# Head pairs of a fused three-layer kernel: later source tiles added on VectorE before the products with a constant -1 matrix

## What is computed

```python
z = jnp.einsum('bhqd,bhkd->bhqk', qb, kb).astype(jnp.float32) * SB_SCALE
mask = k_pos < q_pos
log_1m_beta = jnp.where(mask, -jax.nn.softplus(z), 0.0)
suffix = lax.cumsum(log_1m_beta, axis=3, reverse=True) - log_1m_beta
w = jnp.where(mask, jnp.exp(jax.nn.log_sigmoid(z) + suffix), 0.0)
outs.append(jnp.einsum('bhqk,bhkd->bhqd', w.astype(vb.dtype), vb))
```

## Time and profile before

| | before |
|---|---|
| median of 3 runs (lowest to highest) | 1312.52 us (1311.21 to 1314.37) |
| the profiled execution: its time, and its span | 1313.82 us, 1312.1 us |
| PE busy | 1266.3 us, 97% of the span |
| DVE, ACT, POOL busy | 645.4, 572.5, 398.7 us |
| granted clock of PE, mean | 0.986 of full speed |
| head stage: from its first DVE instruction to its end | 763.4 to 1029 us, eight steps of 33.0 or 33.7 us |

### The profile page before, as it was taken

The page is one execution under the profiler, slowest core; times in us unless marked ns, Lnnn a source line. Parts: engine busy times, 40 slices in busy tenths (PEclk is TensorE's granted clock), DMA queues, the critical chain, the costliest instruction groups (busy, mean ns, idle before and its releaser), DMA issues.

```text
span 1312.1 us, 19522 instructions
## 1 busy us (share of the span) xinstructions
PE 1266.3 (97%) x7802; PEld 1049.3 (80%) x7802; DVE 645.4 (49%) x1208; ACT 572.5 (44%) x1086; POOL 398.7 (30%) x194
## 2 busy tenths in 40 slices
PE   6999998999989999999999999999999999999998
PEld 5799876998968766656699988887877888888898
DVE  6373054485884646789847133333333391102534
ACT  4435313443331227688856343545354311434333
POOL 1454301224544211110020432222222354444441
PEclk9999998999989999999999999999999999999999
DMA  5322200733584331110012331212122223233221
GB/s 174 125 70 91 96 1 32 257 111 119 174 225 83 66 79 33 33 33 1 2 33 69 93 95 60 61 56 64 57 65 63 90 98 94 90 98 111 82 91 65
DMA packets 130209, 109.68 MB, mean 84 GB/s; under 512 B 36162, under 2 KB 127424, under 8 KB 130128
## 3 DMA queue, kind: packets, MB, share of 16 engines
q1 hardware_dynamic: 130128, 108.54, 27.9%
HBM read 106.43 MB, written 2.10 MB: 83 GB/s over the span
## 4 chain that ended last, share of the span: by engine, by line
PE 68%; issue 18%; POOL 7%; DVE 4%; ACT 2%; DMA 0%; POOLq 0%; DVEq 0%; ACTq 0%
PE banks L1135 33%; POOL w_lo L565 6%; PE banks L1126 6%; PE banks L1158 5%; PE banks L1683 3%; PE banks L1535 3%; PE banks L1552 3%; PE banks L1567 3%; PE banks L1223 2%; PE banks L1590 2%; PE banks L1646 2%; PE banks L1697 1%; PE banks L1727 1%; PE banks L1102 1%; DVE w_lo L1793 1%
## 5 line engine op out<-in xcount | busy, mean ns | idle before, releaser
L565 POOL TENSOR_TENSOR w_lo<-raw,w_hi 128x1024 fp32r<-128x1024 f32 x158 | 388.1, 2478 | 821.7 <-ACT w_hi L638 821.6
L1135 PE MATMUL banks<-act_hi,w_hi 128*128 128x512 f32 x704 | 280.8, 399 | 5.8 <-POOL w_lo L565 5.8
L1135 PE MATMUL banks<-act_hi,w_lo 128*128 128x512 f32 x704 | 276.1, 392 | 0.0
L1135 PE MATMUL banks<-act_lo,w_hi 128*128 128x512 f32 x704 | 276.0, 392 | 0.0
L638 ACT ACTIVATE w_hi<-raw 128x1024 fp32r<-128x1024 f32 x168 | 168.1, 1050 | 145.0 <-PE banks L1135 98.7
L1135 PEld LDWEIGHTS banks<-act_hi,w_hi 128*128 128x128 f32 x704 | 133.4, 189 | 36.0 <-issue 8.7
L1135 PEld LDWEIGHTS banks<-act_hi,w_lo 128*128 128x128 f32 x704 | 133.4, 190 | 28.4 <-issue 1.4
L1135 PEld LDWEIGHTS banks<-act_lo,w_hi 128*128 128x128 f32 x704 | 133.3, 189 | 28.3
L1126 PE MATMUL banks<-w_hi,act_hi 128*128 128x256 f32 x384 | 109.1, 284 | 0.0
L1126 PE MATMUL banks<-w_hi,act_lo 128*128 128x256 f32 x384 | 108.7, 283 | 0.0
L1126 PE MATMUL banks<-w_lo,act_hi 128*128 128x256 f32 x384 | 108.7, 283 | 0.0
(11 more groups left out here) (362 smaller groups left out, 2441.0 us busy)
## 6 DMA issues: line engine op xcount, KB each, us to landing
raw<-w_in SPq DMA_DIRECT2D x32, 1024.0 KB, 5.7
raw<-gla_w_in SPq DMA_DIRECT2D x13, 1024.0 KB, 5.3
ada_raw<-w_ada SPq DMA_DIRECT2D x8, 1024.0 KB, 5.7
raw<-nsa_w_in SPq DMA_DIRECT2D x32, 256.0 KB, 4.6
raw<-nsa_w_in SPq DMA_DIRECT2D x7, 1024.0 KB, 5.1
raw<-gla_w_out SPq DMA_DIRECT2D x4, 1024.0 KB, 8.1
ada_first<-w_ada SPq DMA_DIRECT2D x4, 1024.0 KB, 7.3
raw<-nsa_w_out SPq DMA_DIRECT2D x16, 256.0 KB, 4.6
```

Of the source, the lines that this page charges most:

```text
L565: pool.tensor_tensor(w_lo[:, u, k], raw[:, u, k], w_hi[:, u, k].bitcast(F32), ALU.subtract).then_inc(lo_done, 1)
L1135: mm = pe.matmul(b[:], w[:, u, k, m * P:(m + 1) * P], x[:, k, :], start=(k == 0 and n == 0), stop=(k == KT - 1 and n == 2))
```

## The change

On DVE, the sums over later source tiles are made in float32 as soon as groups 1 and 2 are ready: `last_two` is tile 2 plus tile 3 for query tile 3; `later` has two query tiles for source tile 0: for query tile 2 it is tile 1 + tile 2, for query tile 3 tile 1 + `last_two`. They are split into parts, and only then group 0 gets its softplus. On PE every earlier zone takes one product with `minus_r` for each query tile and part instead of one for each later tile: 16 products of 128 columns and 4 of 256 instead of the 24. The products with `tri_r` are the same 16. The new tiles lie in memory that is free in this stage (the last tile of `br_lo` and `br_hi`, and `rstd`).

```diff
+        later = over("later", [P, 2, 2, P], br_lo, at=br_lo.manual_sbuf_range[1] - 4 * S)
+        later_lo = over("later_lo", [P, 2, 2, P], br_lo, F32R, at=br_lo.manual_sbuf_range[1] - 4 * S)
+        later_hi = over("later_hi", [P, 2, 2, P], br_hi, F32R, at=br_hi.manual_sbuf_range[1] - 4 * S)
+        last_two = over("last_two", [P, 2, P], rstd)
...
                 pe.wait_ge(sp_ready, 3 * (p + 1))
-                for jt in range(TT - 1, -1, -1):
-                    for a in range(2):
-                        for st in range(jt, -1, -1):
-                            for n, part in enumerate((sp_hi, sp_lo)):
-                                mm = pe.matmul(blocks(z_banks, a, st, skip=jt - st), (tri_r if jt == st else minus_r)[:],
-                                               blocks(part, a, jt), start=False, stop=(jt == st and n == 1), skip_group_check=True)
-                    if jt < TT - 1:
-                        mm.then_inc(tri_full, 1)
...
+                own(3)
+                sums(lambda a: column(a, 2, 3), minus_r, piece(3, 3))
+                own(2)
+                sums(lambda a: column(a, 1, 2), minus_r, piece(2, 2)).then_inc(tri_full, 1)
+                sums(lambda a: column(a, 1, 3), minus_r, [lambda a, x=x: x[:, a] for x in (last_two_hi, last_two_lo)])
+                own(1)
+                sums(lambda a: column(a, 0, 1), minus_r, piece(1, 1)).then_inc(tri_full, 1)
+                sums(lambda a: column(a, 0, 2, 2), minus_r,
+                     [lambda a, x=x: x[:, a].rearrange("p t n -> p (t n)") for x in (later_hi, later_lo)])
+                own(0).then_inc(tri_full, 1)
...
-                    dve.tensor_tensor(group(sp_lo, g), group(ln_z, g), group(sp_hi, g).bitcast(F32),
-                                      ALU.subtract).then_inc(sp_ready, 1)
...
+                softplus(0, 1)
+                softplus(1, 2)
+                if p:
+                    dve.wait_ge(tri_full, 3 * p)
+                tile2 = ln_z[:, 4].rearrange("p (a t n) -> p a t n", a=2, t=2)
+                link(dve.tensor_tensor(last_two[:], tile2[:, :, 1], ln_z[:, 2:4, 3 * P:], ALU.add))
+                dve.tensor_tensor(later[:, :, 0], tile2[:, :, 0], ln_z[:, 2:4, P:2 * P], ALU.add)
+                link(dve.tensor_tensor(later[:, :, 1], last_two[:], ln_z[:, 2:4, 2 * P:3 * P], ALU.add))
+                softplus_low(1).then_inc(sp_ready, 1)
+                softplus_low(2).then_inc(sp_ready, 1)
+                dve.tensor_copy(last_two_hi[:], last_two[:])
+                link(dve.tensor_copy(later_hi[:], later[:]))
+                dve.tensor_tensor(last_two_lo[:], last_two[:], last_two_hi[:].bitcast(F32), ALU.subtract)
+                link(dve.tensor_tensor(later_lo[:], later[:], later_hi[:].bitcast(F32), ALU.subtract))
+                softplus(2, 0)
+                softplus_low(0).then_inc(sp_ready, 1)
```

More of the change, by code:

```diff
@@ L238, in build_program @@
         w_z = over("w_z", [P, 5, S], sp_hi)
+        later = over("later", [P, 2, 2, P], br_lo, at=br_lo.manual_sbuf_range[1] - 4 * S)
+        later_lo = over("later_lo", [P, 2, 2, P], br_lo, F32R, at=br_lo.manual_sbuf_range[1] - 4 * S)
+        later_hi = over("later_hi", [P, 2, 2, P], br_hi, F32R, at=br_hi.manual_sbuf_range[1] - 4 * S)
+        last_two = over("last_two", [P, 2, P], rstd)
+        last_two_lo = over("last_two_lo", [P, 2, P], rstd, F32R)
+        last_two_hi = over("last_two_hi", [P, 2, P], rstd, F32R, at=last_two.manual_sbuf_range[1])
         pool_u = over("pool_u", [P, KT, S], qh)
@@ L1678, in head_sums, with sums, own, column @@
                 pe.wait_ge(sp_ready, 3 * (p + 1))
-                for jt in range(TT - 1, -1, -1):
-                    for a in range(2):
-                        for st in range(jt, -1, -1):
-                            for n, part in enumerate((sp_hi, sp_lo)):
-                                mm = pe.matmul(blocks(z_banks, a, st, skip=jt - st), (tri_r if jt == st else minus_r)[:],
-                                               blocks(part, a, jt), start=False, stop=(jt == st and n == 1), skip_group_check=True)
-                    if jt < TT - 1:
-                        mm.then_inc(tri_full, 1)
+                def sums(zones, weights, hi_lo, last=False):
+                    for n, part in enumerate(hi_lo):
+                        for a in range(2):
+                            mm = pe.matmul(zones(a), weights[:], part(a), start=False, stop=(last and n == 1),
+                                           skip_group_check=True)
+                    return mm
+                def own(st):
+                    return sums(lambda a: blocks(z_banks, a, st), tri_r,
+                                [lambda a, x=x: blocks(x, a, st) for x in (sp_hi, sp_lo)], last=True)
+                def column(a, st, first, n=1):
+                    at, c0 = zone(a, st)
+                    return z_banks[:, at, c0 + (first - st) * P:c0 + (first - st + n) * P]
+                def piece(st, first):
+                    def of(x, a):
+                        at, c0 = zone(a, st)
+                        return x[:, at, c0 + (first - st) * P:c0 + (first - st + 1) * P]
+                    return [lambda a, x=x: of(x, a) for x in (sp_hi, sp_lo)]
+                own(3)
[8 more added lines that the diff above has]
+                own(0).then_inc(tri_full, 1)
             def head_values(p):
@@ L2192, in _, with softplus @@
                     dve.tensor_scalar(group(ln_z, g), group(z_banks, g), CAP, None, ALU.min).then_inc(zc_ready, 1)
-                for i, g in enumerate((1, 2, 0)):
+                def softplus(i, g):
                     dve.wait_ge(l_ready, 3 * p + i + 1)
@@ L2197, in _, with softplus_low @@
                     link(dve.tensor_copy(group(sp_hi, g), group(ln_z, g)))
-                    dve.tensor_tensor(group(sp_lo, g), group(ln_z, g), group(sp_hi, g).bitcast(F32),
-                                      ALU.subtract).then_inc(sp_ready, 1)
+                def softplus_low(g):
+                    return dve.tensor_tensor(group(sp_lo, g), group(ln_z, g), group(sp_hi, g).bitcast(F32), ALU.subtract)
+                softplus(0, 1)
[14 more added lines that the diff above has]
+                softplus_low(0).then_inc(sp_ready, 1)
                 if p:
```

## The result

| | before | changed |
|---|---|---|
| median (lowest to highest) | 1313.44 us (1311.21 to 1317.04, 4 runs) | 1336.02 us (1333.71 to 1338.54, 4 runs) |
| profiled execution: time, span | 1313.82, 1312.1 us | 1336.79, 1335.0 us |
| granted clock, mean | 0.986 | 0.976 |

The changed kernel takes 1.0172 times as long, 95% interval 1.0153 to 1.0192: 22.6 us slower. The prediction had 13.5 us slower and a range that ended at 1332 us. The direction was right, the size was not.

The account below looks back on a forecast made before the run. PE was taken to bound the kernel, busy 1266.3 of 1312.1 us. Products -6.0, stalls +14.55 and +0.7, clock +4.2 gave +13.5 us on a median of 1312.52: 1326.0 us, range 1310 to 1332.

Parts of the forecast that it names:

- Step 1: PE's sums in the head stage: fewer products, priced by count over columns, gain 0.75 us a pair, 6.0 us in eight.
- Step 2: DVE in the head stage: seven new instructions add 2.97 us a pair ahead of group 0, alone hidden in 4.24 us.
- Step 3: Group 0 on DVE alternates with POOL's subtractions; PE stalls 2.91 us in five pairs, 0.24 in three: 14.55 plus 0.7 us.
- DVE first: Rival: group 0's rounding precedes POOL in the five pairs, stalls of only 0.6 us, 1310.2 us; 11 in 100.
- no wait of the rounding: Rival: group 0's rounding does not wait for POOL, hardly any stall, -5.6 us, 1306.9 us; 10 in 100.
- Step 4: PE's clock falls behind the five long stalls, 0 to 1.7 us more each; half taken, 4.2 us.
- all five stalls bring a fall: Rival: PE's clock falls behind every one of the five long stalls, 8.5 us, +17.8 in all, 1330.3 us; 18 in 100.

Follow-up runs that it names:

- e1: Changed kernel with one more wait on ACT, so that POOL's subtractions start after DVE's group 0: 1308.25 us, ratio to before 0.9968.
- e7: Kernel before with e1's ACT wait and ten dead DVE additions ahead of group 0: 1347.82 us, ratio 1.0269.
- e9: Changed kernel with `head_sums` of the kernel before on PE; DVE's new work stays but is not read: 1334.57 us, ratio 1.0172.
- e10: Kernel of e1 with six dead linked DVE additions ahead of group 0: 1356.92 us, ratio 1.0348.
- e8: Kernel before with e1's ACT wait, three dead DVE additions, and PE waiting for group 0 ahead of chunk c+1's wide products: 1350.03 us, ratio 1.0286.
- e4: Changed kernel with each of POOL's two subtraction instructions cut in two: 1303.35 us, ratio 0.9931.
- e12: Kernel before with each of POOL's two subtraction instructions cut in two, nothing else: 1303.61 us, ratio 0.9929.

## Why the prediction was right in kind and wrong in size

- **Step 1, the products.** 0.75 us a pair forecast, 0.69 measured: 5.5 us instead of 6.0. The price by width, counts over columns, held: the sums of the first pair take 4.81 us in e1 where they took 5.54. The formula of the Trainium skill that the prediction set beside it (N/2.4 + 2.5 ns, "TensorE: Matmul & The Clock Gate", section "Back-to-back issue gap") would have given 6.9 us, by estimate. That section states it for a product without the budget of its weight load, which the prediction left out, and gives about 81 ns a product of 128 columns for a stream of weight loads and products; the rows have 111 ns, so neither figure fits this stream.
- **Step 2, DVE's new work.** 2.97 us forecast. In the third pair of the changed kernel the rounding of group 0 starts at 847.81; the rounding of group 1 had started at 839.92, which is 1.25 us behind the first maximum. So it comes 9.14 us behind it; forecast 9.13.
- **Step 3, the collision.** Rounding 2.75 forecast, 2.77 measured; subtraction 3.36 and 3.27; stall 2.91 and 2.95 in five pairs, 0.24 and 0.3 in three; 15.3 us in all and 15.6. As the waits read a little more than they cost, PE was delayed by some 14.3 us. The pattern of one far-off row in the first layer carried over to within 0.1 us. Both rivals that rested on another order of turns (DVE first, no wait of the rounding) are refuted by the rows above; the rounding does wait.
- **Step 4, PE's clock, is the step that failed.** It put "from 0 to 1.7 us more" on each of the five stalls and took half, 4.2 us. Measured: 14.0 us, 1.4 to 4.4 us a stall. The upper bound came from one fall near the kernel's start, with products of 512 columns behind it, and was taken as the most that one stall can cost:

```profile
20.57 0.63 PE L1278 MATMUL banks<-act_lo,w_hi 128*128 128x512 f32 x1
```

One stall can cost more, in the old sums too: the first fall of e7 and of e9 cost 3.0 us each. With the old sums behind the same stalls (e9) the clock took 6.4 us in all, 2.2 more than the forecast term; the other 7.6 us came with the new sums, so with the change itself. The forecast did name "the sums with their narrow products", but as an argument for more falls, and never as one for longer ones. The rival "all five stalls bring a fall" was right about their number, and 5.5 us too low for the same reason. With 14.0 in place of 4.2 the forecast's sum is -6.0 + 15.3 + 14.0 = +23.3 us, against 22.6 measured. With every term as measured it is -5.5 + 15.6 + 14.0 = 24.1 us, which is what the stage is longer in the table; in the profiled executions the stage also began 1.1 us earlier than before (762.30 for 763.38), and that makes their difference of 23.0 us.
- Trace and page on the clock: the Trainium skill ("TensorE: Matmul & The Clock Gate", section "What's actually happening") has the throttled state as the default and activity as what ends it. The falls in this stage agree, in that each came during or behind an idle time of PE and ended while PE worked. What the clock took behind equal stalls still differed, 12.6 us with the old sums and 23.8 with the new, with PE busy all the time in the rows at 0.50.

## To carry to other kernels

Work that is hidden by its length alone is not yet hidden: look at which engine it will run beside, for every instruction that moves as well as for every new one. Here 3 us of DVE work fitted into 4.2 us of slack, and pushed two old instructions under POOL's; one wait on ACT that delays POOL, free by itself, turned 22.6 us of loss into 4 us of gain. And a stall of PE should be charged with its clock, at a price taken from a stall that has the same kind of products behind it.

## What the runs showed of the hardware that was not expected

- Behind equal stalls the clock costs differ by what follows: e7 and e10, 12.6 and 23.8 us for 23.1 and 23.6 us of waiting; e9 and the changed kernel, 6.4 and 14.0 us for 15.6 us each. The new sums have 20 products of 128 columns out of 36, the old 16 out of 40, and none with `minus_r` and 384 columns is left. What in them makes the difference was not tried.
- Stalls of 0.3, 0.8 and 1.05 us were never followed by a lowered clock, those of 1.7 us in two pairs of five. Of the stalls of 2.5 to 3.5 us nearly all were, 36 of 40 in seven profiles: one in e9 (2.95 us), one in e10 (2.57 us) and two in e8 (3.50 and 2.67 us) were not. A stall of this length makes a fall likely and does not fix it.
- In the rows of these runs VectorE and GpSimd took turns by single instructions, so halving GpSimd's instructions made VectorE's waits half as long (e4). That cut alone gained 9 us in the kernel before (e12).
